# Decoder block pair: the time-step strip in two matmuls a k-tile with two gate strips beside it, the first gate product ahead of the scan, three weight refills subtracted by VectorE

## The reference, cut to what matters

```python
h = rms_norm(x, mix_pre_g)                       # the pre norm
proj = h @ w_in                                  # 1024 x 10272
u_glu, z, xbc, dt_raw, gate = split(proj)        # dt_raw: 32 columns
val, gt = split(u_glu + glu_b)
v = val * sigmoid(gt)                            # 8 tiles of 128 features
v = causal_depthwise_conv(v, dw_w, dw_b)         # 31 taps a feature
dt = softplus(dt_raw + dt_bias)
a = -exp(a_log)
a_cs = cumsum(dt * a) within each chunk          # "the scan"
```

## Time and profile before

| what | value |
|---|---|
| median of 3 runs | 1924.39 us (1921.95 to 1924.89) |
| the profiled execution | 1923.32 us, span 1921.5 us |
| TensorE busy | 1884.3 us, 98% of the span |
| TensorE weight loads | 1551.6 us, 81% |
| VectorE busy | 1025.0 us, 53% |
| ScalarE busy | 1085.0 us, 56% |
| GpSimd busy | 255.9 us, 13% |
| mean granted TensorE clock | 0.995 |
| HBM read | 334.27 MB |

### The profile page before, as it was taken

One profiled execution on the slowest core, in us unless ns is written; L12 is line 12 of the kernel. 1 busy time (PEld: TensorE's weight loads), 2 busy tenths in 40 slices (PEclk: granted clock), 3 DMA queues, 4 the chain that ended last, 5 costly groups with the idle time before them and its releaser, 6 DMA issues.

```text
span 1921.5 us, 26190 instructions
## 1 busy us (share of the span) xinstructions
PE 1884.3 (98%) x9286; PEld 1551.6 (81%) x9286; DVE 1025.0 (53%) x1695; ACT 1085.0 (56%) x1512; POOL 255.9 (13%) x299
## 2 busy tenths in 40 slices
PE   7999999999999999999999999999999999999999
PEld 6877788887888888878878888888888878888886
DVE  5566663455413233358878888788633273133134
ACT  7655666535433333554589997798574544344343
POOL 0110011100111111111111111111111101111110
PEclk9999999999999999989999999999999989999999
DMA  7854468854989898869787778877889839989884
GB/s 231 192 133 109 121 177 201 180 111 114 192 192 193 196 191 193 192 133 212 177 188 185 174 170 212 205 170 173 220 184 200 187 94 211 191 196 191 195 177 114
DMA packets 94346, 339.99 MB, mean 177 GB/s; under 512 B 10488, under 2 KB 10488, under 8 KB 93984
## 3 DMA queue, kind: packets, MB, share of 16 engines
q0 software_dynamic: 42480, 153.64, 44.2%
q1 hardware_dynamic: 47232, 169.14, 30.8%
q10 hardware_dynamic: 4528, 15.81, 2.3%
HBM read 334.27 MB, written 4.28 MB: 176 GB/s over the span
## 4 chain that ended last, share of the span: by engine, by line
PE 80%; DVE 9%; ACT 4%; DMA 3%; issue 2%; ACTq 1%; DVEq 1%; SPq 0%
PE bank L390 20%; PE bank L392 20%; PE bank L391 20%; DVE ssum L2119 5%; PE bank L515 2%; PE bank L516 2%; PE bank L517 2%; DMA wl<-in_weights 1%; PE work L470 1%; PE bank L405 1%; PE bank L407 1%; PE bank L406 1%; DMA raw<-in_weights 1%; ACT wl L993 1%; PE work L685 1%
## 5 line engine op out<-in xcount | busy, mean ns | idle before, releaser
L992 ACT ACTIVATE wh<-raw 128x1024 fp32r<-128x1024 f32 x295 | 312.2, 1058 | 593.7 <-PE bank L392 511.4
L390 PE MATMUL bank<-XAh,wh 128*128 128x512 f32 x1384 | 546.4, 395 | 11.4 <-DVE XAl L1605 8.5
L392 PE MATMUL bank<-XAh,wl 128*128 128x512 f32 x1384 | 540.0, 390 | 0.0
L391 PE MATMUL bank<-XAl,wh 128*128 128x512 f32 x1384 | 539.9, 390 | 0.0
L972 POOL DMA_DIRECT2D wl<-in_weights x295 | 255.7, 867 | 1636.4 <-ACT wl L993 1600.1
L390 PEld LDWEIGHTS bank<-XAh,wh 128*128 128x128 f32 x1384 | 260.5, 188 | 68.8 <-DVE wl L1545 8.7
L993 ACT ACTIVATE wl<-raw 128x1024 fp32r<-128x1024 f32 x295 | 307.8, 1043 | 0.0
L392 PEld LDWEIGHTS bank<-XAh,wl 128*128 128x128 f32 x1384 | 260.5, 188 | 55.5
L391 PEld LDWEIGHTS bank<-XAl,wh 128*128 128x128 f32 x1384 | 260.7, 188 | 53.5 <-issue 0.7
L390 PE MATMUL bank<-XBh,wh 128*128 128x512 f32 x720 | 281.4, 391 | 0.4 <-DVE wl L1552 0.4
L392 PE MATMUL bank<-XBh,wl 128*128 128x512 f32 x720 | 280.2, 389 | 0.0
(11 more groups left out here) (371 smaller groups left out, 2122.2 us busy)
## 6 DMA issues: line engine op xcount, KB each, us to landing
raw<-in_weights SPq DMA_DIRECT2D x294, 512.0 KB, 5.9
wl<-in_weights POOLq DMA_DIRECT2D x287, 512.0 KB, 7.9
arena<-scratch ACTq DMA_DIRECT2D x20, 512.0 KB, 5.5
wraw<-in_weights SPq DMA_DIRECT2D x12, 512.0 KB, 7.0
raw<-in_weights SPq DMA_DIRECT2D x8, 384.0 KB, 4.4
wl<-in_weights POOLq DMA_DIRECT2D x8, 384.0 KB, 6.0
h<-in_xT SPq DMA_DIRECT2D x4, 512.0 KB, 6.7
spill<-cst ACTq DMA_DIRECT2D x8, 256.0 KB, 6.8
```

The costliest lines, as they stand in the source:

```text
L390: mm(bank[s][:, 0:w], hi, tile(X[0], k, w), start=(n == 0), stop=False)
L391: mm(bank[s][:, 0:w], hi, tile(X[1], k, w), start=False, stop=False)
L392: last = mm(bank[s][:, 0:w], lo, tile(X[0], k, w), start=False, stop=(n == len(kts) - 1))
L992: act_(wh[j % 4][:, :], raw[a % 2][:, :], ACT.Copy)
```

## The change

- `dt` has 32 columns, so its low part fits beside its high part in the same 128 columns: VectorE copies the low part's 32 columns of each k-tile to columns 32 to 63 of `wh` (`low_beside`, ahead of the reciprocal of the final norm), and the strip takes two matmuls a k-tile instead of three. The result has the high parts' product in rows 0 to 31 and the low part's in rows 32 to 63, and VectorE adds them.
- dt, glu+0 and glu+1 run side by side; before, dt and glu+0 did.
- ScalarE's refills behind dt, glu+0 and glu+1 (strips 137, 138, 139) all stand ahead of the Exp, and their low parts are computed by VectorE (`LOCAL` has three entries more), ahead of the softplus. GpSimd issues three loads less.
- The first glu product (tile 0) stands ahead of the scan on VectorE; on ScalarE the first sigmoid stands ahead of the wait for the scan, and the refill with strip 140 behind it.

```diff
-LOCAL = [AT["xo"] + n for n in range(4, 8)] + [AT["gu0"] + n for n in range(4, 7)]
+LOCAL = [AT["xo"] + n for n in range(4, 8)] + [AT["glu"] + n for n in range(3, 6)] + [AT["gu0"] + n for n in range(4, 7)]
...
-            def strips_abreast(j, count, X, xn):
+            def strips_abreast(j, count, X, xn, thin=None):
 
                 for n in range(j, j + count):
-                    low_ready(n)
+                    if n == thin:
+                        pe.wait_ge(sem("thin"), 2)
+                    else:
+                        low_ready(n)
...
                         mm(bank[s][:, :], hi, tile(X[0], k), start=(k == 0), stop=False)
-                        mm(bank[s][:, :], hi, tile(X[1], k), start=False, stop=False)
-                        last = mm(bank[s][:, :], lo, tile(X[0], k), start=False, stop=(k == KT - 1))
+                        last = mm(bank[s][:, :], hi, tile(X[1], k), start=False, stop=(n == thin and k == KT - 1))
+                        if n != thin:
+                            last = mm(bank[s][:, :], lo, tile(X[0], k), start=False, stop=(k == KT - 1))
...
-            strips_abreast(AT["dt"], 2, XA, tiles_from("pre"))
-            for n in range(1, 2 * KT):
+            strips_abreast(AT["dt"], 3, XA, tiles_from("pre"), thin=AT["dt"])
+            for n in range(2, 2 * KT):
                 strip(AT["glu"] + n, XA)
...
             step(AT["dt"])
             step(AT["glu"])
+            step(AT["glu"] + 1)
             act.wait_ge(sem("s_abs"), 1)
...
             act.wait_ge(sem("s_one"), 1)
             act_(xt[0:NSH, 1, :], xt[0:NSH, 1, :], ACT.Ln).then_inc(sem("s_exp"), 1)
-            act.wait_ge(sem("s_acs"), 1)
-            act.dma_start(scratch, acs[0:NSH, :]).then_inc(sem("acs_out"), 16)
             for n in range(2 * KT):
                 j, t = AT["glu"] + n, n // 2
-                if n:
+                if n > 1:
                     step(j)
...
                     act.drain().then_inc(bank_free[j % 4], 1)
+                    if t == 0:
+                        act.wait_ge(sem("s_acs"), 1)
+                        act.dma_start(scratch, acs[0:NSH, :]).then_inc(sem("acs_out"), 16)
...
+            def low_beside(j, n):
+
+                dve.wait_ge(w_lo[j % 4], 16 * lows(j))
+                hi, lo = [a[j % 4].rearrange("p (k n) -> p k n", k=KT) for a in (wh, wl)]
+                copy(hi[:, :, 32:32 + n], lo[:, :, 0:n].bitcast(F32))
+                dve.drain().then_inc(sem("thin"), 1)
...
             dve.drain().then_inc(ssum_rdy, 1)
+            low_beside(AT["dt"], NSH)
             cols_recip(NORM["final"])
...
             ps = taken(AT["dt"])
-            leave(TS(acs[0:NSH, :], ps[0:NSH, :], V("dt_b")[0:NSH, :], None, ALU.add), AT["dt"])
+            copy(acs[0:NSH, :], ps[32:32 + NSH, :])
+            dve.drain()
+            leave(TTop(acs[0:NSH, :], acs[0:NSH, :], ps[0:NSH, :], ALU.add), AT["dt"])
+            dve.drain()
+            TS(acs[0:NSH, :], acs[0:NSH, :], V("dt_b")[0:NSH, :], None, ALU.add)
             dve.drain()
             STT(xt[0:NSH, 0, :], acs[0:NSH, :], -1.0, acs[0:NSH, :], ALU.mult, ALU.max)
             dve.drain().then_inc(sem("s_abs"), 1)
+            for n in (3, 4, 5):
+                sub_local(AT["glu"] + n)
             one_plus(NSH, xt[:, 0, :], xt[:, 1, :], sem("s_exp"), sem("s_one"))
             log_one_plus(NSH, xt[:, 0, :], xt[:, 1, :], sem("s_exp"))
+
+            def glu_gate(t):
+
+                j = AT["glu"] + 2 * t
+                dve.wait_ge(bank_free[(j + 1) % 4], (j + 1) // 4 + 1)
+                ps = taken(j)
+                v = vpad[:, t, CONV_K - 1:]
+                leave(STT(v, ps[:, :], V("glu_b", t), sq[:, t % 2, :], ALU.add, ALU.mult), j)
+                dve.drain().then_inc(sem("glu_v"), 1)
+
+            glu_gate(0)
             STT(xt[0:NSH, 1, :], acs[0:NSH, :], 0.0, xt[0:NSH, 1, :], ALU.max, ALU.add)
```

More of the change, by code:

```diff
@@ L417, in strips_abreast @@
                     pe.wait_ge(x_ready, xn[k] + 1)
-                    for s in [n % 4 for n in range(j, j + count)]:
+                    for n in range(j, j + count):
+                        s = n % 4
                         hi, lo = wh[s][:, k * P:(k + 1) * P], wl[s][:, k * P:(k + 1) * P]
                         mm(bank[s][:, :], hi, tile(X[0], k), start=(k == 0), stop=False)
-                        mm(bank[s][:, :], hi, tile(X[1], k), start=False, stop=False)
-                        last = mm(bank[s][:, :], lo, tile(X[0], k), start=False, stop=(k == KT - 1))
+                        last = mm(bank[s][:, :], hi, tile(X[1], k), start=False, stop=(n == thin and k == KT - 1))
+                        if n != thin:
+                            last = mm(bank[s][:, :], lo, tile(X[0], k), start=False, stop=(k == KT - 1))
                         if k == KT - 1:
@@ L1841, in _ @@
                 elif n == 6:
[L1842 to L1846, removed]
+                    low_beside(AT["hgrn"] + n + 2, FH)
                 elif n == 9:
@@ L2131, in _ @@
             for t in range(KT):
[L2132 to L2137, removed]
+                if t:
+                    glu_gate(t)
                 for _ in range(glu_parts[t]):
```

## The result

The changed kernel takes 1928.79 us (median of 6 runs) where the one before takes 1921.93 (6 runs): ratio 1.0035, 95% interval 1.0025 to 1.0045. Run again beside other kernels it gave 1.0031 (1.0020 to 1.0042, 8 runs). By the ratios it is 6.0 to 6.7 us slower; the forecast was +4.7. Two executions in the slow state, one of 6620.08 us in experiment 8 and one of 2100.83 us of the kernel before, are left out of the ratios. One profiled execution took 1927.16, 3.8 more than that of before. It had reached the first matmul of the stage at 830.36 instead of 832.44 (code ahead of the stage, the same in both but for the cast, and the first steps of the chain at a higher clock: eight short matmuls took 1.13 us instead of 2.04). So I count from that matmul: from there to the end it needs 1925.3 - 830.36 = 1094.9 us, before it was 1921.5 - 832.44 = 1089.1, so 5.9 more.

A forecast was written before the change was run, and what follows sets the result against it. TensorE, busy nearly throughout, was taken to bound the kernel. Matmuls -1.8, cast +0.2 and some 6.3 of new waits made +4.7 on a 1924.39 us median: 1929.1 us, range 1926.0 to 1931.5.

The forecast's parts named there:

- glu+4: TensorE's fifth glu strip, held for VectorE's first gate product: start at 864.4 against 862.21, 2.2 us later.
- The bounds given for the change: Bounds for the main forecast alone, from cast, dt chain and landing: +4.2 to +5.8, 1928.6 to 1930.2 us.
- D: Rival: transfers late; no. 140 lands 2 us later, or third refill 4.0 and clock falls; glu+6 +5.5 to +7; chance 0.15.
- The wait: TensorE, ready at 860.3, stands 4.1 us ahead of glu+4 until VectorE's gate product is done.
- The matmuls saved: Eight fewer TensorE matmuls for the dt strip at 0.227 us each: 1.8 us off.
- The cast: One 128x256 VectorE cast ahead of the first reciprocal: 0.30 us plus drain, moving the stage's start 0.2 later.
- The dt chain: VectorE's copy, add, bias add and maximum behind the dt strip, with drains: 2.9 us, ending at 851.2.
- the raw load: Third refill's 512 KB load, issued after VectorE's first subtraction: 3.3 us to land, at 856.0 (upper bound 856.7).
- The fall of the clock: TensorE's clock may fall in the wait ahead of glu+4: 2.2 us, putting glu+6 at +4.4, still under VectorE's delay.
- VectorE's 4.7: VectorE's depthwise taps start at 866.9 against 862.21 without slack, so glu+14 starts 4.7 us later, at 921.4.
- The low load of no. 140: Low part of strip 140's refill lands 7.0 us after issue, at 876.7, starting glu+6 3.6 us later.
- Three side by side: Three strips side by side at the stage's start fill no gap, since TensorE never waits after the first tile.

The follow-up runs named there:

- experiment 8: Changed kernel with the fourth refill (strip 140) moved ahead of ScalarE's wait for the scan; ratio 1.0023.
- Experiment 5: Kernel before with only its third refill (strip 139) moved ahead of Exp on ScalarE; ratio 1.0008 (0.9999 to 1.0018).
- 3: Changed kernel with VectorE's first subtraction (strip 137) ahead of the dt chain instead of behind it; 1926.41 us, ratio 1.0033.
- 2: Changed kernel with refills 139 and 140 behind the first sigmoid and the subtraction for 139 behind the scan; 1926.69 us, ratio 1.0028.
- 10: Changed kernel: refills 139, 140 behind first sigmoid, third subtraction ahead of scan, four taps moved from glu tile 4 to group 4's end; 1921.83 us, ratio 1.0000.
- 9: Kernel before with only four VectorE taps moved from glu tile 4 to the last slot of group 4; ratio 0.9993 (0.9984 to 1.0002).
- 11: Changed kernel with 15 extra matmuls, strip glu+3's first five k-tiles multiplied twice to fill the wait ahead of glu+4; ratio 1.0038.
- 1: Changed kernel reduced to the thin dt strip: two strips side by side, no VectorE subtractions, refills, gate and scan in the old order; ratio 1.0001.
- 4: Changed kernel with the first gate product behind the scan and the first sigmoid behind the wait for it, as before; 1928.39 us, ratio 1.0040.
- 12: Changed kernel run again without alteration, against the kernel before; ratio 1.0031 (1.0020 to 1.0042).
- 6: Kernel before plus thin dt strip, first gate product and sigmoid ahead of the scan, third refill behind that sigmoid; 1919.74 us, ratio 0.9986.

## Why the prediction was right, and where it was off

*Direction and mechanism.* Right. The third refill stands ahead of Exp on ScalarE and of the softplus on VectorE, its raw load waits for VectorE's first subtraction, and glu+4 waits for the gate. Experiment 5 shows the wait that the order alone makes (2.3 us in its profile; the times leave its price open), 3 that the wait goes with the time at which the raw buffer is free, 2 that it is gone when the order is undone. The order and the taps together (10) bring the time from 1.0035 to 1.0000, of which the taps alone (9) may be 0.0007.

*The number.* The time was forecast at 1929.1 and measured at 1928.79, and that closeness is luck. The forecast stood on a median of three runs of the kernel before, 1924.39; six runs gave 1921.93. The base was 2.5 too high and the change, +4.7 for the 6.9 between the medians, 2.2 too low. The bounds given for the change, +4.2 to +5.8, did not hold it. The range set out from the better base would be 1923.5 to 1929.0 and would still hold the time, by its upper end, which is D's.

*Times up to glu+4.* Counted from the first matmul, whose start contains the cast, glu+4 was forecast at 864.4 - 832.6 = 31.8; it was 31.6 and 32.0. The wait was forecast at 4.1; it was 3.9. The matmuls saved 1.9 in one profile and 1.5 in the other (forecast 1.8). The cast took 0.29 (0.30). The dt chain took 2.8 (2.9), the raw load 3.3 us to land (3.3).

*The fall of the clock.* Forecast as possible, at 2.2 us, and kept out of the sum, where VectorE's 4.7 covered it; it came, at 1.6 in the changed kernel (7.2 us for glu+4 where before it took 5.5), and 11 shows that it goes with the standstill. By the rule of the Trainium skill, TensorE: Matmul & The Clock Gate, section "What's actually happening", a throttle is the resting state and activity releases it, and the profiles agree: clock 0.57 behind the wait, 1.00 where the wait was filled. It doesn't come at every wait, and the length of one doesn't tell: those of 2.1 and 1.9 us in experiment 3 left the clock up; one of 1.9 in 10, one of 2.4 in 2 and one of 2.3 in 5 did not.

*The low load of no. 140: the term that was mis-sized.* I took 7.0 us to land from a load that had one other beside it for its first four microseconds. It had three others beside it within 2 us, and took 9.0 (9.2 in the second profile). The trace of before already showed this: of the seven low loads that GpSimd issued from 847 to 878, the landing took 6.7 to 9.6 us, and the 9.6 is that of 865.78, issued 2.1 us behind another low load. The 7.0 was the second shortest of them. In the sum a fall of the clock and a wait at glu+6 cover each other: with 7.0 us the load would have landed at 874.3, ahead of TensorE at 874.8. With 9.0 they add. I had kept 7.0 in the sum and put the late landing among the rivals (D), at a chance of 0.15: it is D's condition that held, by 2 us, and its price of +5.5 to +7 at glu+6 is close to the +5.3 and +5.7 there (46.1 and 46.5 against 40.7). The change in time, 6.0 to 6.7 by the ratios, lies inside it.

*Which run decides at glu+14.* I had VectorE's taps at +4.7. They started 4.5 late (34.3 against 29.8), but the sixth gate product ended at 917.49 + 0.75 - 830.36 = 87.9, before at 84.1: +3.8, because small pauses between VectorE's taps, which the timeline of before has (0.45 us ahead of 864.04, 0.43 ahead of 911.56), were gone. TensorE, at +5.4, had passed it. Experiment 8 shows the forecast's bound when the low load is taken away: +4.2 at glu+14.

*The sum.* 1.9 by the wait at glu+4 less what the thin strip saves, 1.6 by the clock, 1.8 by the low load (the wait of 1.6 and a slower start behind it) make 5.3 at glu+6 and 5.4 at the end of the glu strips. 0.3 come in the groups: the last MLP starts 5.7 late (714.8 against 709.1). Then 1.2 come back, by the clock and not by the change: behind the norm's wait, which is 4.8 us in both, it stays at 1.2 GHz for 5.6 us before and for 3.1 in the changed kernel's profile. The low load in the last MLP costs 1.2, which makes 5.7; the profile has 5.9. The two medians are 6.9 and 5.7 above those of before, the ratios say 6.7 and 6.0; what lies between is inside their scatter.

*Three side by side.* I called it worth nothing, because TensorE lags behind the tiles. For the six matmuls a k-tile of before that holds. For the five of a thin strip with one other it doesn't: in 1 TensorE waits for the tiles and has 0.9 of the 1.8 us left.

## What to carry to other kernels

A refill that is issued earlier than its buffer can be loaded turns a prefetch into a wait, and everything behind it in that engine's queue pays, here Exp, the gate, the scan and the next refill. Before moving an issue up, ask when its data can be there, and who frees the buffer. And where one wait is put into a stage whose transfers are near their limit, the refills behind it come together and land later than a quiet row says: price them from the row with the most neighbours. Last, compare the forecast of a change with the measured change, not one time with another: a base that is off can hide that the change was.

## What the runs showed of the hardware

- A wait of TensorE of 2.3 to 7.6 us ahead of a strip was followed by a fall to the 1.2 GHz level in 2, 4, 5, 8, 11 and both profiles of the changed kernel, and so was one of 1.9 us in 10. The strip behind it took 7.0 to 7.2 us instead of 5.4 to 5.5, 1.6 or 1.7 more, and in 11 2.7 more. Waits of 1.9 and 2.1 us in 3 and of 1.7 in 12, at glu+6, were not.
- The same code can go either way. At 264 us, in code that is the same in all kernels here, TensorE waits for a low load: 1.86 us in 12 and 1.96 in 1, where the granted clock then was 0.50 from 265.5 to 268.5 and 0.56 from 262.5 to 266.0. It was 1.85 in before and 2.14 in 6, and the clock stayed up.
- A 512 KB load that is added to its target landed after 6.7 to 9.6 us in the kernel before, from 847 to 878 us, and after 9.0 and 9.2 in the two profiles of the changed kernel with three others issued within 2 us; a plain one with none issued beside it after 3.3.
- An ACTIVATE that rounds a strip behind a table load for Ln needed no new table load (857.25 in the earlier trace rows), and a table load is started before the semaphore that its ACTIVATE waits for: in 2 that for Ln starts at 850.98 and Ln at 854.26, 2.00 us of it idle and ended by VectorE.
